# Quarter-array products for the sample streams' state, and filler products on TensorE, in the RWKV-7 recurrence of a two-layer encoder step

## The reference, cut to what matters

```
S = S * w_t + (S @ a_t) b_t^T + v_t k_t^T        # 64 x 64 state per head
y_t = S @ r_t
```

## Time and profile before

| | us |
|---|---|
| median of 3 runs | 2306.42 (2304.41 to 2319.5) |
| the profiled execution, its own time | 2300.22 |
| its span from first to last instruction | 2298.4 |
| busy: PE, DVE, ACT, POOL | 2064.6, 1332.8, 747.0, 198.3 |
| mean granted TensorE clock, share of full | 0.925 |

### The profile page before, as it was taken

How to read it: one execution, slowest core, us unless ns; L and a number is a source line. 1 busy time by engine, 2 the same in 40 slices (tenths; PEclk the granted TensorE clock), 3 DMA queues, 4 the chain that set the end, 5 groups by cost and what they waited for, 6 DMA issues and landing times.

```text
span 2298.4 us, 37193 instructions
## 1 busy us (share of the span) xinstructions
PE 2064.6 (90%) x15388; PEld 1915.2 (83%) x15388; DVE 1332.8 (58%) x2123; ACT 747.0 (32%) x1290; POOL 198.3 (9%) x199
## 2 busy tenths in 40 slices
PE   2989988888888979899999998998778989999996
PEld 2988876667667759899999998998557989999996
DVE  7665566666666434876427745343554687526754
ACT  3443443333333322422112214222664422212222
POOL 2000223220222000000000000001320000000000
PEclk9999878777878859999999999999999999999998
DMA  2211000000000022122222122242542122222121
GB/s 111 91 66 44 11 1 13 12 7 8 13 11 12 12 96 76 45 85 72 69 88 74 61 68 74 83 151 91 212 150 76 72 74 70 69 83 74 67 69 58
DMA packets 30325, 150.69 MB, mean 66 GB/s; under 512 B 4784, under 2 KB 7600, under 8 KB 17872
## 3 DMA queue, kind: packets, MB, share of 16 engines
q1 hardware_dynamic: 30160, 148.32, 18.6%
HBM read 137.84 MB, written 10.47 MB: 65 GB/s over the span
## 4 chain that ended last, share of the span: by engine, by line
PE 58%; DVE 7%; ACT 3%; issue 2%; DMA 0%; DVEq 0%; ACTq 0%; POOL 0%; SPq 0%; POOLq 0%
PE ps L593 16%; PE ps L594 16%; PE ps L595 16%; PE ps L1936 1%; PE ps L1907 1%; PE ps L659 1%; PE ps L658 1%; PE ps L657 1%; DVE prob L2085 1%; ACT prob L1978 1%; ACT prob_t L1988 1%; DVE w_lo L588 1%; PE ps L1317 1%; PE ps L1916 1%; DVE split_f L804 1%
## 5 line engine op out<-in xcount | busy, mean ns | idle before, releaser
L593 PE MATMUL ps<-x_hi,w_hi 128*128 128x320 f32 x2208 | 692.8, 314 | 67.3 <-DVE x_lo L711 41.3
L594 PE MATMUL ps<-x_lo,w_hi 128*128 128x320 f32 x2208 | 689.5, 312 | 0.0
L595 PE MATMUL ps<-x_hi,w_lo 128*128 128x320 f32 x2208 | 688.9, 312 | 0.0
L593 PEld LDWEIGHTS ps<-x_hi,w_hi 128*128 128x128 f32 x2208 | 421.1, 191 | 72.4 <-issue 46.9
L588 DVE TENSOR_TENSOR w_lo<-raw,w_hi 128x2048 fp32r<-128x2048 f32 (+2 forms) x110 | 229.7, 2089 | 410.1 <-ACT w_hi L582 410.1
L594 PEld LDWEIGHTS ps<-x_lo,w_hi 128*128 128x128 f32 x2208 | 421.3, 191 | 0.2
L595 PEld LDWEIGHTS ps<-x_hi,w_lo 128*128 128x128 f32 x2208 | 421.0, 191 | 0.0
L582 ACT ACTIVATE w_hi<-raw 128x2048 fp32r<-128x2048 f32 (+2 forms) x110 | 192.0, 1745 | 419.6 <-PE ps L595 419.6
L593 PE MATMUL ps<-hid_hi,w_hi 128*128 128x320 f32 x704 | 217.5, 309 | 0.0
L594 PE MATMUL ps<-hid_lo,w_hi 128*128 128x320 f32 x704 | 217.5, 309 | 0.0
L595 PE MATMUL ps<-hid_hi,w_lo 128*128 128x320 f32 x704 | 217.5, 309 | 0.0
(11 more groups left out here) (263 smaller groups left out, 3121.6 us busy)
## 6 DMA issues: line engine op xcount, KB each, us to landing
raw<-in_w_gate SPq DMA_DIRECT2D x22, 1024.0 KB, 4.8
raw<-in_w_up SPq DMA_DIRECT2D x22, 1024.0 KB, 4.8
raw<-in_w_down SPq DMA_DIRECT2D x16, 768.0 KB, 4.2
raw<-in_w_down SPq DMA_DIRECT2D x16, 640.0 KB, 3.9
raw<-in_w_kv SPq DMA_DIRECT2D x8, 1024.0 KB, 4.8
past_k<-in_past_k SPq DMA_DIRECT2D x8, 1024.0 KB, 4.8
past_v<-in_past_v SPq DMA_DIRECT2D x8, 1024.0 KB, 4.9
raw<-in_w_r SPq DMA_DIRECT2D x4, 1024.0 KB, 6.9
```

The lines of the kernel that those rows point to most:

```text
L593: pe.matmul(out, w, x, start=start, stop=False)
L594: pe.matmul(out, w, xl, start=False, stop=False)
L595: return pe.matmul(out, wl, x, start=False, stop=stop)
```

## The change

The sample streams' part is laid on quarters and halves of the 128 x 128 array:

- "s_from": instead of 8 products with 128 rows (both heads, the other one zeroed) to 64 outputs by 64 columns, 16 products of 64 rows to 64 outputs by 32 columns, each head on its own rows and outputs, straight from `ra`. `s_ar`, POOL's two instructions for it and the waits on it are gone. ACT's copy to `s_from` is 128 x 256 instead of 64 x 512.
- "s_pre" and "s_out": one product of `s_from` with the full 128 x 128 identity in the place of two of 64 x 64.
- "s_state": one step, in slot 14, in the place of slots 10 and 13. `spread` is [2, 2, 4, 64]: a token's values lie at its stream's place among the four of its half (g). 8 products of 64 rows (a half of the tokens) to 64 outputs (a head) by 256 columns take the place of 4 products of 128 rows to 64 outputs by 512 columns; half g goes to bank 4 or 7. POOL and DVE make `spread` once for both heads (slots 6 and 8), DVE adds to `state_s` in two instructions of 128 x 256 in slot 14.

And `pe_filler`, a product of the identity with 256 columns of the table into a bank that PE has just claimed and that the next product overwrites, is issued 19 times in each of rounds 0 to 7: before the grams of token tiles 1 to 4, before each of the three "bk_tok" groups, and before part 0 of the six "inv" and six "add" of levels 1 to 6.

```diff
+    def pe_filler(pe, bank, n=2 * P):
+        pe.matmul(ps[:, bank, 0:n], ident, table[:, 0:n], start=True, stop=True)
...
             banks = [claim(pe, ("gram", f, hh, u)) for hh in range(2)]
+            if u:
+                pe_filler(pe, banks[0])
...
             bank = claim(pe, ("bk_tok", f, j))
+            pe_filler(pe, bank)
...
             if phase == "inv":
-                pe.wait_ge(S("inv_packed"), 2 * ((len(LEVELS) - 1) * f + n - 1) + part + 1)
                 key = ("inv", f, part, n)
                 bank = claim(pe, key)
+                if part == 0:
+                    pe_filler(pe, bank)
+                pe.wait_ge(S("inv_packed"), 2 * ((len(LEVELS) - 1) * f + n - 1) + part + 1)
...
+                banks = [claim(pe, ("add", f, part, hh, n)) for hh in range(2)]
+                if part == 0 and n:
+                    pe_filler(pe, banks[0])
                 emptied(pe, ("off", f, part, n))
-                banks = [claim(pe, ("add", f, part, hh, n)) for hh in range(2)]
...
             elif step == "s_from":
-                pe.wait_ge(S("s_ar_made"), f + 1)
                 bank = claim(pe, ("s_from", f))
                 for s in range(NS):
-                    mm = pe.matmul(ps[0:HD, bank, s * 4 * TS:(s + 1) * 4 * TS].rearrange("p (c t) -> p c t", c=4), state_s[:, s, :],
-                                   s_ar[:, :, :, s * TS:(s + 1) * TS].rearrange("p h q t -> p (h q) t"), start=True, stop=True)
+                    for hh in range(2):
+                        rows = slice(hh * HD, (hh + 1) * HD)
+                        mm = pe.matmul(ps[rows, bank, s * 2 * TS:(s + 1) * 2 * TS].rearrange("p (q t) -> p q t", q=2), state_s[rows, s, :],
+                                       ra[rows, b, :, TP + s * TS:TP + (s + 1) * TS], start=True, stop=True)
...
+                pe.matmul(ps[:, bank, 0:P], s_from[:, A_OF, :], ident, start=True, stop=False)
                 for hh in range(2):
-                    out = ps[:, bank, hh * HD:(hh + 1) * HD]
-                    pe.matmul(out, s_from[:, hh, A_OF, :], ident[0:HD, 0:HD], start=True, stop=False)
-                    mm = pe.matmul(out, score(f, hh, SAMPLE, "ka"), v_of(f, SAMPLE, hh), start=False, stop=True)
+                    mm = pe.matmul(ps[:, bank, hh * HD:(hh + 1) * HD], score(f, hh, SAMPLE, "ka"), v_of(f, SAMPLE, hh), start=False, stop=hh == 1)
...
-                bank = claim(pe, ("s_state", f)) if n == 0 else place[("s_state", f)][0]
-                pe.wait_ge(S("spread_made"), 2 * f + n + 1)
-                pe.wait_ge(S("v_spread_made"), 2 * f + n + 1)
-                out = ps[n * HD:(n + 1) * HD, bank, :].rearrange("p (s i) -> p s i", s=NS)
-                pe.matmul(out, bk_tok[:, b, SAMPLE, 0, n * HD:(n + 1) * HD], spread[:, 0, :, :], start=True, stop=False)
-                mm = pe.matmul(out, bk_tok[:, b, SAMPLE, 1, n * HD:(n + 1) * HD], spread[:, 1, :, :], start=False, stop=True)
+                banks = [claim(pe, ("s_state", f, g)) for g in range(2)]
+                pe.wait_ge(S("spread_made"), f + 1)
+                pe.wait_ge(S("v_spread_made"), f + 1)
+                for q in range(2):
+                    for g, bank in enumerate(banks):
+                        rows = slice(g * HD, (g + 1) * HD)
+                        for hh in range(2):
+                            out = ps[hh * HD:(hh + 1) * HD, bank, 0:HALF_STATES].rearrange("p (s i) -> p s i", s=NS // 2)
+                            mm = pe.matmul(out, bk_tok[rows, b, SAMPLE, q, hh * HD:(hh + 1) * HD], spread[rows, q, hh, :, :],
+                                           start=q == 0, stop=q == 1)
...
-            for hh in range(2):
-                ins = pool.tensor_scalar(s_ar[:, hh, :, :], ra[:, f % 2, :, TP:T], tab("head")[:, hh:hh + 1], 1.0, MUL, MUL)
-            ins.then_inc(S("s_ar_made"), 1)
...
+            elif step == "s_state":
+                for g in range(2):
+                    bank = filled(dve, ("s_state", f, g))
+                    half = state_s[:, g * NS // 2:(g + 1) * NS // 2, :]
+                    read(dve.tensor_tensor(half, half, ps[:, bank, 0:HALF_STATES].rearrange("p (s i) -> p s i", s=NS // 2), ADD),
+                         ("s_state", f, g))
```

More of the change, by code:

```diff
@@ L26 @@
                    ("keep", T), ("causal", P),
-                  ("stream", NS), ("head", 2),
+                  ("stream", NS // 2), ("head", 2),
                   ("eps_gn", 1), ("log_shift", 1),
@@ L64, in tables @@
     put("causal", np.where(col <= row, 0.0, 1e30))
-    put("stream", row // TS == np.arange(NS)[None, :])
+    put("stream", row // TS % (NS // 2) == np.arange(NS // 2)[None, :])
     put("head", row // HD == np.arange(2)[None, :])
@@ L209, in build @@
     s_v = Space(rec.at, 229344)("s_v", [T])
-    spread = rec("spread", [2, NS, HD])
+    spread = rec("spread", [2, 2, NS // 2, HD])
     stats = rec("stats", [2, NT * 2])
@@ L231, in build @@
     ring0 = in_ring(0)
-    s_ar = ring0("s_ar", [2, 2, NS * TS])
-    s_from = ring0("s_from", [2, 2, NS * TS], rows=HD)
+    s_from = ring0("s_from", [2, NS * TS])
     inv_n = ring0("inv_n", [NT, P])
@@ L366, in build @@
     SAMPLE = NT - 1
+    HALF_STATES = NS // 2 * HD
     PARTS = range(2)
@@ L418, in build @@
             STEPS[3 * (n + 1) + j].append((step, n))
-    for k, step, hh in ((4, "s_from", 0), (6, "s_pre", 0), (7, "s_u", 0), (9, "s_out", 0),
-                        (10, "s_state", 0), (13, "s_state", 1)):
+    for k, step, hh in ((4, "s_from", 0), (6, "s_pre", 0), (7, "s_u", 0), (9, "s_out", 0), (14, "s_state", 0)):
         STEPS[k].append((step, hh))
@@ L464, in build @@
                         take((step, i - 1, n), 4)
-                    elif n == 0:
+                    elif step == "s_state":
+                        for g, bank in enumerate((4, 7)):
+                            take(("s_state", i - 1, g), bank)
+                    else:
                         take((step, i - 1), 5 if step == "s_out" else 7)
@@ L1458, in act_rec @@
             if i == NF and k == 2:
-                filled(act, ("s_state", NF - 2))
+                filled(act, ("s_state", NF - 2, 1))
                 make_hi(act, C_O)
@@ L1539, in act_states @@
                     filled(act, ("s_out", f - 1))
-                read(act.activation(s_from[:, :, :, :].rearrange("p h q (s t) -> p (h q) s t", s=NS),
-                                    ps[0:HD, bank, :].rearrange("p (s c t) -> p c s t", s=NS, c=4), ACT.Copy), ("s_from", f))
+                read(act.activation(s_from[:, :, :].rearrange("p q (s t) -> p q s t", s=NS),
+                                    ps[:, bank, 0:2 * NS * TS].rearrange("p (s q t) -> p q s t", s=NS, q=2), ACT.Copy), ("s_from", f))
             elif step == "s_u":
@@ L1601, in pool_rec, with stream_of_row @@
                 pool_prepare(pool, i + 1, k, chain)
+    def stream_of_row():
+        a = tab("stream")
+        return bass.AP(a.tensor, a.offset, [list(a.ap[0]), [0, 2], [1, NS // 2], [0, HD]])
     def pool_squares(pool, f):
@@ L1822, in dve_states @@
                 read(dve.tensor_copy(su_pre[:, :, :], ps[:, bank, 0:P].rearrange("p (h i) -> p h i", h=2)), ("s_pre", f))
-            elif step == "s_state" and n:
-                bank = filled(dve, ("s_state", f))
-                read(dve.tensor_tensor(state_s[:, :, :], state_s[:, :, :], ps[:, bank, :].rearrange("p (s i) -> p s i", s=NS), ADD),
-                     ("s_state", f))
-        if k in (8, 11):
-            hh = int(k == 11)
+            elif step == "s_state":
+                for g in range(2):
+                    bank = filled(dve, ("s_state", f, g))
+                    half = state_s[:, g * NS // 2:(g + 1) * NS // 2, :]
+                    read(dve.tensor_tensor(half, half, ps[:, bank, 0:HALF_STATES].rearrange("p (s i) -> p s i", s=NS // 2), ADD),
+                         ("s_state", f, g))
+        if k == 8:
             emptied(dve, ("s_u", f))
-            if hh:
-                dve.wait_ge(S("spread_used"), f + 1)
-            elif f:
-                filled(dve, ("s_state", f - 1))
+            if f:
+                filled(dve, ("s_state", f - 1, 1))
                 filled(dve, ("sv_t", f - 1))
-            dve.tensor_tensor(spread[:, 0, :, :], su_tok[:, hh, :].unsqueeze(1).broadcast_to([P, NS, HD]),
-                              tab("stream").unsqueeze(2).broadcast_to([P, NS, HD]), MUL).then_inc(S("spread_made"), 1)
+            dve.tensor_tensor(spread[:, 0, :, :, :], su_tok[:, :, :].unsqueeze(2).broadcast_to([P, 2, NS // 2, HD]),
+                              stream_of_row(), MUL).then_inc(S("spread_made"), 1)
     def dve_centre(dve, f, chain):
@@ L1848, in dve_centre @@
         emptied(dve, ("bonus", f))
-        filled(dve, ("s_state", f))
+        filled(dve, ("s_state", f, 1))
         dve.tensor_tensor(s_v[:, :].rearrange("p (t h i) -> p t h i", t=NT, h=2),
```

34 lines of the change are left out of this document (14 added, 20 removed).

## The result

| | before | changed |
|---|---|---|
| median of 7 runs each, side by side | 2304.41 (2296.94 to 2319.5) | 2288.45 (2282.0 to 2298.61) |
| ratio, 95% interval | | 0.9924 (0.9897 to 0.995) |
| the profiled execution, its span | 2300.22, 2298.4 | 2282.0, 2280.2 |
| mean granted clock | 0.925 | 0.949 |
| the recurrence in it | 601.9 | 587.7 |

The kernel became 16 us faster by the medians, where I had forecast 4 us slower. In the profiled executions the spans differ by 18.2 us: 14.2 in the recurrence, 1.4 ahead of it and 2.6 behind it, where the change does nothing; executions of one kernel spread by more than those 4 us.

What follows compares the result with a forecast made beforehand. PE, busy 90% of the span, bounds it, with the clock low in the recurrence. Rounds 1 to 6 +7, round 0 -2, round 7 +4, round 8 -5: total +4 on 2300.2, plus 6.2 for the median: 2310 us, range 2250 to 2345.

Steps and rivals of the forecast that it cites:

- rival A: Recurrence: the fillers hold the clock, middle round 67.0 us, rounds 1 to 6 -45, time 2260; chance 0.35 with rival D.
- With fillers I expect two of the six rounds 1 to 6: Rounds 1 to 6: two get the clock back earlier, 6 us each; 6 x 3.1 - 2 x 6 = +7 us.
- one step later: Long half-clock stretch of a middle round: the clock rises at filler, "inv" and "out" of level 4, +0.8 us.
- dense streams bring the clock back: Middle round: dense column streams hold the clock, short products with waits lose it; inferred from four clock changes.
- slot 10: "s_state" products removed there: -2.8 us at half clock (7.0 to 4.2), -0.6 at full clock.
- slot 13: "s_state" products removed there: loses 1.86 us at full clock, keeps about 0.8 of wait, -1.0.
- slot 14: Eight quarter products of "s_state" and DVE's adds, ahead of "off" of level 5: nothing hides them, +1.4 us (0.7 to 4).
- the price of a filler: 256 columns: 0.47 us full clock, 0.90 half, plus 0.1 drain; exposed at "add", partly at grams and "bk_tok"; +6.2 a round.
- four quarters side by side: "s_state" in slot 14: eight products of 256 columns overlap on the array's quarters and take about 1.0 us.
- rival C: Slot 14: quarters queue one behind the other, 3.7 us, 2.7 more in eight rounds, +20, time 2330; 0.23 with Rival B.
- Rival B: From slot 10: clock falls as now, not back before next round's logits, +46 us, time 2350; chance 0.23 with rival C.
- Rival D: Fillers cost nothing, only "inv" and "add" waits are filled: middle round -3, time 2282; chance 0.35 with rival A.

Runs made afterwards that it cites:

- e2: The kernel before with the 19 fillers a round added and "inv" claiming its bank ahead of the wait for ACT: 2335.0 us, ratio 1.0125 to before.
- e1: The changed kernel with all four calls of `pe_filler` taken out, so the quarters alone: 2305.69 us, ratio 0.9999 to the kernel before.
- e4: The changed kernel with all 19 fillers, the "add" one issued between the claims of the two heads' banks: 2264.9 us, ratio 0.9826 to before.
- e7: e4 with fillers of 128 columns in the place of 256: 2293.49 us, ratio 0.9951 to the kernel before.
- e8: e4 with fillers of 512 columns in the place of 256: 2266.19 us, ratio 0.9837 to the kernel before.
- e10: e4 with gram fillers between their claims, none at "bk_tok", 512 columns at long "inv" and "add" waits: 2228.39 us, ratio 0.966 to before.
- e11: e4 with fillers on 64 rows of the array, still 256 columns: 2316.03 us, ratio 1.0015 to the kernel before.

## Why the prediction was wrong

The measured 2288 us lies in the range, 22 below the forecast (2310) and 28 above rival A (2260): faster where I had said slower. Split rounds 1 to 6 into a part at full clock and a part lost to the half clock. At full clock a full-length round is 63.7 us before (the stretches of e2's round, 70.1, less its 6.4 of fillers) and 66.2 after. Taking round 1 as 4 us shorter, six are 378 and 393; measured 442.7 and 429.8. So:

| rounds 1 to 6, us | forecast | measured |
|---|---|---|
| more work at full clock | +27 (6 x (67.0 - 62.5)) | +15 (6 x 2.5) |
| less lost to the half clock | -20 (what remains of +7) | -28 (65 to 37) |
| sum | +7 | -13 |

*The step that failed: "With fillers I expect two of the six rounds 1 to 6" to get the clock back, at 6 us each.* Five did: rounds 3 to 6 by most of their loss (71 us, 5 over the full-clock round), round 1 too; round 2 did not at all. So half-clock time went from 265 to 153 us. The working, with the rise "one step later", took the fall as fixed. But of the earlier trace rows's fall at 404.6, 24 us long in rounds 2 to 5 before and 10 in round 6, rounds 3 to 6 have none left, and rounds 1 and 2 keep one, in round 2 with its rise as late as 438.5. That the fillers hold the clock is shown by e2 in the old kernel (265 to 162), and the quarters alone do the opposite (e1, 265 to 396). That the fillers alone remove this fall is not: in e2 each of rounds 2 to 6 still has it, 24.0 us long in three of them and 10.5 in two. It went where fillers and quarters are together, and no run says by which of their stretches. The reading behind the step, that dense streams bring the clock back, is not borne out in round 2 either: the clock came back there behind 28.6 us of short products and 256-column fillers.

*The second: the size of the quarters' gain.* At full clock I had -0.6 for slot 10, -1.0 for slot 13, +1.4 for slot 14, -0.3 and -0.4 for the rest, together -0.9. Measured between e2 and the changed kernel it is -3.9, of which 1.0 is the two "inv" fillers that become hidden once the streams ahead of them are gone; so -2.9 like for like. Slots 10 and 13 gave 1.66 each, 1.1 without that: I had let a longer wait for ACT's pack take the products' place, and only 0.18 us of one is left (500.39, 507.15). Slot 14 cost 1.23, but 0.9 of it came back before the next "add", where the wait for DVE was 2.15 us and is now 1.25: together +0.3, not +1.4. That nothing hides slot 14 was wrong. At half clock slot 10 was put at -2.8, from 7.0 us to 4.2, and it is 4.2 in round 2. Two readings were off besides. The 3.1 us from "add" to "inv" are round 7's; in a middle round they are 4.4 at full clock (487.47 to 491.87, with 1.54 of wait for ACT's `inv_f`), which is most of the way from the text's full-clock round (62.5) to 63.7. And the weight columns of "s_from" are not kept: 8 loads of 64 became 16 of 64 on quarters, which cost nothing (1.08 us in e2, 1.05 in round 2 of the changed kernel).

*Right: the price of a filler and where it is exposed.* At full clock the text has 5.4 us a round; e2 shows 6.4, of which the 1.0 just named is absent in the changed kernel. The step to half-array products is 0.09 to 0.17, inside 0 to 0.25; the "add" filler lies behind its own wait, which e4 confirms by what mending it gives. The gram stage with "bk_tok" cost 2.0 where I had 1.6.

*Right: "s_out" and four quarters side by side.* Eight products in 1.03 us against 1.0; rival C's 3.7 is refuted. "s_out" at half clock is 5.8 us with what stands around it, a filler included, and 6.1 before without one; with 0.9 or 1.0 for the filler that is about -1.2 for the step, where I had -1.1.

*Rival A* has its mechanism shown by e7, e4 and e8, and its full-clock round (67.0 against 66.2). It overshot by 32 us in rounds 1 to 6: 12 for round 2; 17 for rounds 3 to 6, which lost the clock again in the gram stage (14.6 us for logits and grams in round 3 and 15.7 in rounds 4 to 6, 12.9 at full clock) and at "s_from" (476 in round 3); 3 for round 1. The Trainium skill, "TensorE: Matmul & The Clock Gate", section Why this matters for your kernels, advises bursts without idle gaps for the high clock. The falls listed above agree in that each comes in a wait of 0.82 to 2.81 us or within 2.4 us of one; that such a burst brings it back soon does not hold in round 2, where PE is busy 33.03 of 34.10 us at 0.50. *Rival B*, the clock not coming back before the next logits, is half seen in round 2: its half-clock stretch ran 10 us longer than before and ended 9 us ahead of them. e1 shows it in full (0.50 from 401.7 to 459.7, with the logits at 455.9). *Rival D* (2282) has nearly the time and not the mechanism: fillers do cost.

*Outside rounds 1 to 6.* Round 0 I had at -2: it is +2.2 (45.7 to 47.9), its clock at 0.93 from 0.67. Round 7 I had at +4: -0.1, its clock at 1.00 from 0.88. Round 8 I had at -5: -3.4.

Open: why round 2, with the same instructions as round 3 and the same wait of 1.31 us, falls to the half clock there and stays. The falls of rounds 3 to 6 lie at other places, and one profile of each kernel can't tell chance from a pattern.

## What to carry to other kernels

Where short products alternate with waits, an edit that takes out work can lose by the clock all that it saves (e1), and must be costed at both levels of the clock. Here it took out a long stream of columns and lengthened waits; which of the two lost the clock is not separated. A filler pays if it is issued ahead of the wait and not behind it, so ask which semaphore the claim of its bank really waits for (e4), and give each the length of its wait (e10): the same idea went from 0.992 to 0.966 by place, size and three fillers a round fewer. A filler on 64 of the rows won nothing (e11, 1.0015).

## What the runs showed of the hardware

- PE busy for 33.03 of 34.10 us stayed at 1.2 GHz; being busy for that long did not bring the clock back.
- Fillers of 128, 256 and 512 columns at the same 19 places left 287, 135 and 43 us of half clock in the recurrence.
- A float32 product of 64 x 64 and 256 columns on each quarter of the array: eight in 1.03 us, where one of the whole array with 256 columns takes 0.43 to 0.51 to the next transpose.
- The step from a whole-array product to half-array ones cost 0.09 to 0.17 us.
- Fillers of 256 columns on 128 rows with 64 outputs left 100 us of half clock, full ones 135, and ones on 64 rows with 128 outputs 272.
